# Products of the identity in TensorE's pauses, in a hybrid attention, recurrence and expert layer

## The chip, the cores and the metric

One core of one Trainium2 chip runs the whole program. The metric is the device time of one execution in microseconds (us), from runs of the same program; beside it stands one execution taken by the hardware profiler. TensorE has a clock that a throttle grants; the profile gives it as a share of 2.4 GHz, and it has two levels, 0.50 (1.2 GHz) and 1.00 (2.4 GHz).

## What is computed

One layer on x of 2048 tokens by 1024 columns, float32:

```
proj = x @ w_in                       # 2464 columns: c_q 256, c_kv 128, k_r 32, f, i, q, g 512 each
a = rms_norm(mla(c_q, c_kv, k_r))     # 8 heads, low-rank q and kv, rotary key, block-causal mask of 64
r = hgrn2(f, i, q, g)                 # 4 heads of 128, gated recurrence over chunks
h = layer_norm(ALPHA * x + concat(a, r) @ w_out)
moe: group = argmax(h @ w_router_group)          # 4 groups, top 1
     experts = top 2 of the 8 of that group      # 32 experts of 1024 x 512 (w1, w3) and 512 x 1024 (w2)
     y = (silu(h @ w1[e]) * (h @ w3[e])) @ w2[e], weighted by the gates and added
out = layer_norm(ALPHA * h + moe)
```

## The kernel before

The program is five blocks (stages) in sequence. Inside a block each engine has its own instruction list, in the order written, and engines meet through semaphores; at the end of a block all engines meet before any of them starts the next block. Float32 matrices are split into a high and a low part (type F32R), and a product is made of three such products (high by high, low by high, high by low). Products whose operands are plain F32 are one instruction in the code.

- **First stage, phase_a.** Eight spans of 256 tokens: projections, the chunkwise recurrence and its norm. Then the columns of the attention group are projected for all spans (project_four), and after each the sums of squares are taken with a matrix of ones (sums, L448; products at L453, bank pb or pu). The last thing on TensorE is sums(NS - 1). VectorE ends with the rotary factors and their product with the shared key (L777). Behind the block stand the clearing of semaphores and a barrier (L779, L780).
- **Second stage, phase_b.** TensorE first folds the shared key (L995, four products into S), then runs PROLOGUE, four preparations: keys, queries, values, queries of the first head (project, L1018; the values are the loop at L1033, four products of 128 columns per call, the queries two products of 512 columns). Then a loop over groups of steps: scores (L1051 to L1053, each of three products), transposes of the probabilities into T (L1063), the weighing of values (L1083), folds of the output (L1089), and the preparations for later heads. A score waits for the low part of the queries, which GpSimd writes (L1196) from what ScalarE (L1140) and VectorE (L1232) made of the prologue's banks. SyncE stores the outputs and waits until all have landed (L987).
- **Third stage, phase_c.** For each of eight pairs of 128-token tiles: w_out times attention and recurrence output (share, L1508), residual and layer norm on VectorE, the addition of the bias on GpSimd (L1664), and then the routing logits: route (L1537, eight transposes of h into H), copies of these by VectorE (L1673) and ScalarE (L1599), and logits (L1545, eight products of 36 columns into L). Its opening, begin (L1554), needs the split output weights: ScalarE writes the high part, VectorE the low part wo_lo (L1752 for the first four, L1749 for the last four, once their loads have landed); its first transposes are turn_a (L1527, into A[0]), whose low part VectorE writes behind wo_lo. The loop over pairs leaves logits(NT - 2, 0), route(NT - 1, 1) and logits(NT - 1, 1) for behind it. Rounds of the choice of experts for earlier pairs run on VectorE inside the loop.
- **Routing, phase_d.** A chain of small steps on VectorE (Chain: each waits for the one before) for the last four tiles and then for all: choose gives both, the mask of the two experts of each token; TensorE multiplies it with a triangle and with ones for the ranks (L1889, L1890), VectorE works out blocks and places up to at_blk (L1829, two halves), TensorE makes 32 products of 98 columns, the tokens (L1895, into tk), and one for the list of experts (L1898); VectorE makes at_gate of these (L1852, four instructions), and TensorE 32 products of 196 columns, the shares (L1902, into sh), which VectorE copies (L1875, L1876). SyncE meanwhile loads the first expert's weights, GpSimd gathers the first rows of h.
- **Expert stage and last norm, phase_e.** Rounds of 128 (and tails of 64) gathered tokens through one expert each, weights loaded for each round, then the last layer norm. Here TensorE is the engine with no idle time. At the opening it transposes the gathered rows (L2174) and those of the first tail (L2184, L2186).

The change adds its products to the lists of TensorE in the first four blocks. The instructions between which they stand: after sums(NS - 1) in phase_a; between the loop over PROLOGUE and the loop over groups, and behind the latter, in phase_b; ahead of begin(), between the loop of pairs and logits(NT - 2, 0), and at the end, in phase_c; and at four places in phase_d, ahead of each wait on steps but that for full, and at the end.

In the whole kernel t["ident"] is a plain F32 matrix of 128 by 128, t["ones"] as well. The values' projection is, for comparison, the same form of instruction as the added ones (F32, stationary 128x128, 128 columns):

```
for i in range(4):
    ins = pe.matmul(b[:, i * P:(i + 1) * P], t["ckvn"][:, (4 * c + i) * P:(4 * c + i + 1) * P],
                    wv[:, g], start=True, stop=True)
```

So is the product of keys and queries in the first stage, four heads for each of two halves of a span (L384):

```
for i in range(2):
    for h in range(HG):
        ins = pe.matmul(U[i][:, h * P:(h + 1) * P], key[:, h, i * P:(i + 1) * P],
                        ep[:, h, i * P:(i + 1) * P], start=True, stop=True)
```

Of the kernel before, what the change touches and what calls it, by code (L numbers as in the profile page):

```python
# [20 lines left out]
F32 = mybir.dt.float32  # L21
# [7 lines left out]
P = 128  # L29
# [73 lines left out]
def since(eng, sem, count):  # L103


    if not isinstance(count, int) or count > 0:
        eng.wait_ge(sem, count)


def shape_constants():  # L110
# [61 lines left out]
def phase_a(nc, t, d):  # L172

    with ExitStack() as ctx:
# [37 lines left out]
        O = psum("po")  # L212
# [35 lines left out]
        with nc.Block() as block:  # L248
# [53 lines left out]
            def _(pe):  # L302
# [143 lines left out]
                def sums(j):  # L446

                    pe.wait_ge(c_raw, 3 * j + 3)  # L448
                    pe.wait_ge(c_sq, 3 * j + 3)
                    b = PAIR[j % 2][0]  # L450
                    for n, (lo, hi) in enumerate(((0, 1), (1, 3))):
                        for k in range(lo, hi):
                            ins = pe.matmul(b[:, n * SPAN:(n + 1) * SPAN], t["ones"][:], csq[:, j % 2, k, :], start=(k == lo), stop=(k == hi - 1))  # L453
                    ins.then_inc(c_sum, 1)

                spans(pe, span)
                for j in range(1, NS):
# [9 lines left out]
                    sums(j - 1)  # L467
                    project_four(PAIR[j % 2], C_COLS, j % 2, c_done, 8, 16)
                sums(NS - 1)

            @block.scalar
            def _(act):
# [428 lines left out]
def phase_b(nc, t, d):  # L901


    with ExitStack() as ctx:
# [24 lines left out]
        T = [psum(f"pT{i}") for i in range(NTB)]  # L929
        O = [psum(f"pO{i}") for i in range(2)]  # L930
# [32 lines left out]
        with nc.Block() as block:  # L963
# [26 lines left out]
            def _(pe):  # L990
# [101 lines left out]

                for p in PROLOGUE:
                    project(p)
                for g in range(NGR + 2):
                    for half in range(2):
                        for n, i in scores_in(g, half):
                            score(n, i)
                        for s in slots_in(g, half):
                            if s < NU:  # L1100
                                turn(s)
                            if LAG <= s < NU + LAG:
                                weigh(s - LAG)
                            if s in FOLD_SLOT:
                                fold(FOLD_SLOT[s])
                        for p in preps_in(g, half):
                            project(p)

            @block.scalar
            def _(act):  # L1110
# [273 lines left out]
def phase_c(nc, t, d):  # L1384


    with ExitStack() as ctx:
# [21 lines left out]
        A = [psum(f"cA{i}") for i in range(1)]  # L1409
# [41 lines left out]
        with nc.Block() as block:  # L1451
# [39 lines left out]
            def _(pe):  # L1491
# [72 lines left out]
                def step(m, first):  # L1564
                    turn_a(m, 0)
                    project(m, 0)
                    if not first:
                        logits(m * 2 - 2, 0)
                        route(m * 2 - 1, 1)
                        if not isinstance(m, int) or m > 1:  # L1570
                            ranks(m - 2)
                    project(m, 1)
                    if not first:
                        logits(m * 2 - 1, 1)
                    route(m * 2, 0)
                begin()
                pe.wait_ge(c_loaded, 2 * 16)
                step(1, False)
                pe.wait_ge(r_consts, 3 * 16)
                with pe.Fori(2, STEPS) as m:  # L1580
                    step(m, False)
                logits(NT - 2, 0)
                route(NT - 1, 1)
                logits(NT - 1, 1)

            @block.scalar
            def _(act):
# [178 lines left out]
def phase_d(nc, t, d):  # L1766


    with ExitStack() as ctx:
# [14 lines left out]
        tk = ctx.enter_context(nc.psum_tensor("dT", [P, 512], F32))  # L1784
        sh = ctx.enter_context(nc.psum_tensor("dS", [P, 512], F32))
        xr = ctx.enter_context(nc.psum_tensor("dX", [P, 512], F32))
        listed = sem("d_listed"); copied = sem("residual_copied"); steps = sem("dve_d_steps"); exps = sem("d_exps_done"); ranks = sem("d_ranks")
        tokens = sem("d_tokens"); gates = sem("d_shares")
        idx_ready, gathered = t["idx_ready"], t["gathered"]
# [3 lines left out]
        with nc.Block() as block:  # L1793
# [90 lines left out]

            @block.tensor
            def _(pe):
                pe.wait_ge(steps, at["both"])
                b = s["both"][:].rearrange("p n e -> p (n e)")
                pe.matmul(rk[:, 0].rearrange("p n e -> p (n e)"), t["before"][:], b, start=True, stop=True)  # L1889
                pe.matmul(rk[:, 1].rearrange("p n e -> p (n e)"), t["ones"][:], b, start=True, stop=True).then_inc(ranks, 1)  # L1890

                for k in range(2):
                    pe.wait_ge(steps, at[f"at_blk{k}"])
                    for n in range(NT):
                        ins = pe.matmul(tk[:, 0:NBP], t["at_tok"][:, k, n], at_blk[:, k, n], start=(k == 0 and n == 0), stop=(k == 1 and n == NT - 1))  # L1895
                ins.then_inc(tokens, 1)
                pe.wait_ge(steps, at["full"])
                pe.matmul(xr[0:1, 0:P], full[:], t["ident"][:], start=True, stop=True).then_inc(listed, 1)  # L1898
                for k in range(2):
                    pe.wait_ge(steps, at[f"at_gate{k}"])  # L1900
                    for n in range(NT):
                        ins = pe.matmul(sh[:, 0:2 * NBP], t["at_row"][:, k, n], at_gate[:, k, n].rearrange("p f b -> p (f b)"),  # L1902
                                        start=(k == 0 and n == 0), stop=(k == 1 and n == NT - 1))
                ins.then_inc(gates, 1)

            @block.gpsimd
            def _(pool):
# [774 lines left out]
```

## Time and profile before

| what | value |
|---|---|
| median of 3 runs | 2335.55 us (2334.26 to 2335.8) |
| the profiled execution, its time | 2333.03 us |
| the profiled execution, its span (first to last instruction) | 2331.2 us |
| mean granted TensorE clock | 0.966 |
| PE busy | 2139.4 us, 92% |
| DVE busy | 1650.2 us, 71% |
| ACT busy | 1230.3 us, 53% |
| stages, start in the span | 0, 574.3, 1214.7, 1462.9, 1506.7 us |

PE is TensorE's matmuls, PEld its weight loads, DVE VectorE, ACT ScalarE, POOL GpSimd, SP SyncE. PEclk is the granted clock as a share of 2.4 GHz. A row of the timeline has the start, the time from the first start to the last end, engine, line, operation, what is written <- what is read, the shape and the number of records; in square brackets stands the idle time of the engine before it and what ended that. Records of matmuls overlap: the time of a run of them is the pace times their number, plus one latency.

### The profile page before, as it was taken

Reading aid. Unit: us, or ns where it says so; the run is one execution under the profiler, and the core shown is the slowest. Engines: PE = TensorE matmul, PEld = TensorE weight load, DVE = VectorE, ACT = ScalarE, POOL = GpSimd, SP = SyncE. Lnnn points to the kernel's source line nnn. Section 1 sums busy time; section 2 is a strip of 40 time slices with the busy share of each in tenths; the row PEclk is TensorE's granted clock in tenths of the full one; section 3 lists DMA queues with packets and bytes.
Section 4 is the critical chain, followed back from the end, with each engine's and each line's share of the span. In section 5 each row is a group of like instructions: output and inputs, shape, how many; then the busy total and the mean of one; then the engine's idle time right before and its main releaser. Section 6 shows DMA issues by size and latency. Waiting matters only on the chain. (4 is left out here: it accounts for less than half of the span.)

```text
span 2331.2 us, 40107 instructions
## 1 busy us (share of the span) xinstructions
PE 2139.4 (92%) x13020; PEld 1810.6 (78%) x13021; DVE 1650.2 (71%) x3068; ACT 1230.3 (53%) x2095; POOL 442.6 (19%) x256
## 2 busy tenths in 40 slices
PE   7999999999899999999989999499999999999980
PEld 6888888898677877787877888378888888888860
DVE  5444444465778878778775787778898877777756
ACT  5333333323666766677663221167676755656645
POOL 0000000000100000000001111124343435444436
PEclk9999999999899999999999999599999999999995
DMA  4111111333000000000034443489999988878937
GB/s 187 64 64 63 63 71 75 124 129 118 4 7 6 18 6 9 14 6 12 7 103 165 145 146 122 170 327 368 361 380 378 354 309 280 283 266 286 344 88 292
DMA packets 82215, 361.95 MB, mean 155 GB/s; under 512 B 25824, under 2 KB 37856, under 8 KB 65952
## 3 DMA queue, kind: packets, MB, share of 16 engines
q1 hardware_dynamic: 69136, 318.88, 36.2%
q0 software_dynamic: 11520, 41.16, 7.2%
q8 instruction: 68, 1.11, 0.2%
q10 hardware_dynamic: 1440, 0.37, 0.1%
q14 instruction: 51, 0.42, 0.1%
HBM read 291.97 MB, written 68.94 MB: 155 GB/s over the span
## 5 line engine op out<-in xcount | busy, mean ns | idle before, releaser
L2446 DVE TENSOR_TENSOR w_raw<-w_raw,w_hi 128x2048 fp32r<-128x2048 f32 x128 | 286.9, 2282 | 0.0
L1196 POOL TENSOR_TENSOR qT_lo<-q_raw,qT_hi 128x512 fp32r<-128x512 f32 x32 | 41.0, 1280 | 1124.4 <-ACT qT_hi L1140 1124.4
L1159 ACT CAST prT_hi<-pT 128x512 fp32r<-128x512 f32 (+1 forms) x288 | 162.6, 565 | 157.9 <-PE pT L1063 157.0
L1278 DVE TENSOR_TENSOR prT_lo<-pT,prT_hi 128x512 fp32r<-128x512 f32 (+1 forms) x288 | 188.1, 656 | 53.4 <-ACT prT_hi L1159 51.3
L2201 PE MATMUL eH<-w_hi,at_tok 128*128 128x512 f32 x512 | 206.9, 404 | 1.7 <-DVE at_tok L2439 1.7
L2202 PE MATMUL eH<-w_hi,at_tok 128*128 128x512 f32 x512 | 203.6, 398 | 0.0
L1269 DVE TENSOR_REDUCE mx<-pS 128x1 f32<-128x512 f32 (+2 forms) x320 | 191.2, 608 | 13.5 <-PE pS L1053 6.8
L2319 ACT CAST w_hi<-w_raw 128x2048 fp32r<-128x2048 f32 x64 | 122.6, 1916 | 73.9 <-issue 42.0
L99 POOL TENSOR_TENSOR cell<-cell 128x1 f32<-128x1 f32 x66 | 77.6, 1175 | 442.4 <-ACT y L2331 176.3
L1151 ACT ACTIVATE pr<-pS,nmx 128x512 f32<-128x512 f32 (+3 forms) x240 | 151.0, 639 | 14.4 <-DVE nmx L1273 14.0
L1063 PE MATMUL pT<-ident,pr 128*128 128x128 f32 x828 | 150.1, 275 | 8.3 <-DVE prT_lo L1278 8.0
L1051 PE MATMUL pS<-kT_hi,qT_hi 128*128 128x512 f32 (+2 forms) x320 | 137.2, 429 | 20.1 <-POOL qT_lo L1196 7.2
L2446 DVE TENSOR_TENSOR w_raw<-w_raw,at_row 128x2048 fp32r<-128x2048 f32 x62 | 139.2, 2286 | 13.2 <-ACT at_row L2310 12.6
L1083 PE MATMUL pO<-prT_hi,v_split 128*128 128x256 f32 x576 | 135.5, 317 | 2.3 <-DVE a_out L1294 2.3
L2208 PE MATMUL eH<-w_raw,at_tok 128*128 x512 | 129.7, 395 | 0.0
L305 PE MATMUL pb<-xT_hi,wf_hi 128*128 128x256 f32 x352 | 104.0, 295 | 22.0 <-DVE xT_lo L602 20.5
L2310 ACT CAST w_hi<-w_raw 128x2048 fp32r<-128x2048 f32 x64 | 119.3, 1922 | 0.0
L1083 PE MATMUL pO<-prT_lo,v_split 128*128 128x256 f32 (+1 forms) x576 | 118.4, 287 | 0.0
L1053 PE MATMUL pS<-kT_hi,qT_lo 128*128 128x512 f32 (+2 forms) x320 | 117.2, 366 | 0.0
L1052 PE MATMUL pS<-kT_lo,qT_hi 128*128 128x512 f32 (+2 forms) x320 | 117.1, 366 | 0.0
L2201 PEld LDWEIGHTS eH<-w_hi,at_tok 128*128 128x128 f32 x512 | 97.3, 190 | 25.2 <-issue 2.1
L2310 ACT CAST at_row<-w_raw 128x2048 fp32r<-128x2048 f32 x62 | 114.7, 1901 | 0.0
(429 smaller groups left out, 6017.2 us busy)
## 6 DMA issues: line engine op xcount, KB each, us to landing
w_raw<-in_w SPq DMA_DIRECT2D x96, 2048.0 KB, 12.5
xt<-in_x_t SPq DMA_DIRECT2D x9, 1024.0 KB, 7.8
xs<-in_x SPq DMA_DIRECT2D x8, 1024.0 KB, 4.8
scratch_h<-hp SPq DMA_DIRECT2D x16, 512.0 KB, 2.7
scratch_z<-hp SPq DMA_DIRECT2D x16, 512.0 KB, 3.6
fz<-scratch_z SPq DMA_DIRECT2D x16, 512.0 KB, 10.2
out<-fz SPq DMA_DIRECT2D x15, 512.0 KB, 4.2
scratch_xT<-xT_hi SPq DMA_DIRECT2D x7, 1024.0 KB, 3.9
```

The source lines that it names most:

```text
L1051: pe.matmul(b[:, 0:w], qh[:, slot, at], kh[:, key_slot(h), keys], start=True, stop=False)
L1063: ins = pe.transpose(b[:, m * P:(m + 1) * P], probs(n, i)[:, kt * P:(kt + 1) * P], t["ident"][:])
L1083: ins = pe.matmul(o, v[:, 2 * g + kk], w[:, u % RING, at], start=(g == 0 and m == 0), stop=(g == q and m == 3))
L1151: nc.scalar.activation(probs(n, i)[:, j * 512:j * 512 + w], S[S_AT["score", (n, i, j)] % 4][:, 0:w], ACT.Exp, scale=SCALE, bias=nmx[:, til ...
L1159: nc.scalar.copy(ph[:, u % RING, 0:w], T[u % NTB][:, 0:w]).then_inc(t_hi, 1)
L1269: v.tensor_reduce(mx[:, tile % 4, j:j + 1], b[:, 0:w], AX, ALU.max).then_inc(mx_part, 1)
L1278: v.tensor_tensor(pl[:, u % RING, 0:w], T[u % NTB][:, 0:w], ph[:, u % RING, 0:w].bitcast(F32), ALU.subtract).then_inc(t_lo, 1)
L2201: pe.matmul(H[:], xh[:, k, :], w.hi[:, k, :], start=(k == 0), stop=False)
L2202: pe.matmul(H[:], xl[:, k, :], w.hi[:, k, :], start=False, stop=False)
L2208: ins = pe.matmul(H[:], xh[:, k, :], lo[:, k, :], start=False, stop=(k == KT - 1))
L2310: nc.scalar.copy(w.hi[:, at], w.words(side)[:, at].bitcast(F32)).then_inc(w.hi_ready if half else w.hi_half, 1)
L2446: v.tensor_tensor(w.words(side)[:, at], w.words(side)[:, at].bitcast(F32), w.hi[:, at].bitcast(F32), ALU.subtract).then_inc(w.lo_ready if ...
```

## The change

A helper issues count products of a 128x128 matrix by itself into 128 columns of a bank. It is called at ten places with 14, 72, 14, 18, 28, 6, 40, 132, 60 and 20 products (404 in all), with the matrix of ones at the first and the identity at the others. A bank is given that nobody reads from then on or before its next writing; in routing a new one is allocated. No wait or semaphore is added and nothing is moved.

```diff
@@ -105,6 +105,12 @@
+def stay_warm(pe, bank, words, count):
+
+    for _ in range(count):
+        pe.matmul(bank[:, 0:P], words[:], words[:], start=True, stop=True)
@@ -467,6 +473,7 @@
                     project_four(PAIR[j % 2], C_COLS, j % 2, c_done, 8, 16)
                 sums(NS - 1)
+                stay_warm(pe, O, t["ones"], 14)
@@ -1092,6 +1099,7 @@
                 for p in PROLOGUE:
                     project(p)
+                stay_warm(pe, T[0], t["ident"], 72)
                 for g in range(NGR + 2):
@@ -1105,6 +1113,7 @@
                         for p in preps_in(g, half):
                             project(p)
+                stay_warm(pe, T[0], t["ident"], 14)
@@ -1573,15 +1582,18 @@
                     route(m * 2, 0)
+                stay_warm(pe, L, t["ident"], 18)
                 begin()
                 pe.wait_ge(c_loaded, 2 * 16)
                 step(1, False)
                 pe.wait_ge(r_consts, 3 * 16)
                 with pe.Fori(2, STEPS) as m:
                     step(m, False)
+                stay_warm(pe, A[0], t["ident"], 28)
                 logits(NT - 2, 0)
                 route(NT - 1, 1)
                 logits(NT - 1, 1)
+                stay_warm(pe, A[0], t["ident"], 6)
@@ -1784,6 +1796,7 @@
+        spare = ctx.enter_context(nc.psum_tensor("dV", [P, 512], F32))
@@ -1884,11 +1897,13 @@
             def _(pe):
+                stay_warm(pe, spare, t["ident"], 40)
                 pe.wait_ge(steps, at["both"])
                 b = s["both"][:].rearrange("p n e -> p (n e)")
                 pe.matmul(rk[:, 0].rearrange("p n e -> p (n e)"), t["before"][:], b, start=True, stop=True)
                 pe.matmul(rk[:, 1].rearrange("p n e -> p (n e)"), t["ones"][:], b, start=True, stop=True).then_inc(ranks, 1)
 
+                stay_warm(pe, spare, t["ident"], 132)
                 for k in range(2):
                     pe.wait_ge(steps, at[f"at_blk{k}"])
                     for n in range(NT):
@@ -1896,12 +1911,14 @@
                 ins.then_inc(tokens, 1)
                 pe.wait_ge(steps, at["full"])
                 pe.matmul(xr[0:1, 0:P], full[:], t["ident"][:], start=True, stop=True).then_inc(listed, 1)
+                stay_warm(pe, spare, t["ident"], 60)
                 for k in range(2):
                     pe.wait_ge(steps, at[f"at_gate{k}"])
...
                 ins.then_inc(gates, 1)
+                stay_warm(pe, spare, t["ident"], 20)
```

## Rows read from the trace of the kernel before

**Rows 1.** Windows by stage: us, PE, PEld, DVE, ACT, POOL busy (count), PEclk, DMA.

```profile
1462.90:1508.20 45.30, 15.66 (x70) 14.60 (x70) 36.15 (x111) 1.80 (x4) 5.01 (x3) 0.53 0.42 165
...
1530.00:2256.00 726.00, 725.93 (x3394) 588.31 (x3393) 575.95 (x536) 467.79 (x428) 304.42 (x170) 1.00 0.88 314
```

**Rows 2.** One line of the timeline, one of source line L384: F32 products, 128 columns.

```profile
581.22 1.05 PE L1034 MATMUL pS<-wv,ckvn 128*128 128x128 f32 x8
...
L384 PE MATMUL pu<-gate,key x128: 270/275/275, 61.7 to 460.0; 128*128 128x128 f32 x128
```

**Rows 3.** Timeline, end of the first stage.

```profile
570.01 1.53 PE L453 MATMUL pu<-csq,ones 128*128 128x256 f32 x6 [0.84 <-ACT csq L570]
...
574.32 0.43 DVE L1206 TENSOR_TENSOR krp<-krp,trig 128x256 f32<-128x256 f32 x1 [1.09 <-PEq L780]
```

**Rows 4.** Timeline behind the prologue, and the window behind it (columns as in 1).

```profile
582.11 1.88 PE L1031 MATMUL pS<-cqn,wq 128*128 128x512 f32 x4
...
591.19 0.45 PE L1051 MATMUL pS<-kT_hi,qT_hi 128*128 128x128 f32 x1 [7.20 <-POOL qT_lo L1196]
...
591.20:597.00 5.80, 5.80 (x18) 4.25 (x19) 3.34 (x12) 4.65 (x10) 1.27 (x1) 0.50 0.00 0
```

**Rows 5.** Second to third stage: timeline, and SyncE's waits of line L987.

```profile
1210.83 1.28 PE L1089 MATMUL pO<-stack,oT 128*128 128x64 f32 x8
...
L987 SPq EVENT_SEMAPHORE  x2: 17/22/28, 1213.6 to 1214.2; - x2
...
1214.74 0.09 DVE L1739 MEMSET carry<- 128x32 f32 x1 [2.25 <-PEq L963]
...
1217.65 0.76 PE L1508 MATMUL cM<-wo_hi,rts_hi 128*128 128x512 f32 x1 [5.54 <-DVE wo_lo L1752]
...
1229.40 2.47 DVE L1749 SCALAR_TENSOR_TENSOR wo_lo<-hT,ga,wo_hi 128x1024 fp32r<-128x1024 f32 x2
...
1230.54 0.60 PE L1527 MATMUL cA<-ident,an 128*128 128x128 f32 x4
```

**Rows 6.** Third stage's tail: timeline, and two windows (columns as in 1).

```profile
1445.82 1.87 PE L1545 MATMUL cL<-wr,hT 128*128 128x36 f32 x16
...
1452.19 3.63 PE L1545 MATMUL cL<-wr,hT 128*128 128x36 f32 x16 [3.60 <-DVE hT L1673]
...
1455.62 1.95 PE L1537 MATMUL cH<-ident,hp 128*128 128x128 f32 x8
...
1458.29 3.60 PE L1545 MATMUL cL<-wr,hT 128*128 128x36 f32 x16 [0.72 <-issue]
...
1448.60:1450.60 2.00, 0.00 (x0) 0.00 (x0) 1.57 (x5) 0.77 (x2) 0.00 (x0) 0.96 0.00 0
...
1452.20:1461.90 9.70, 8.97 (x40) 8.46 (x40) 0.89 (x2) 0.59 (x1) 1.66 (x1) 0.50 0.27 108
```

**Rows 7.** Timeline of routing and of the ends of its block.

```profile
1462.86 0.09 DVE L1804 MEMSET tok<- 128x34 int32 x1 [0.73 <-PEq L1451]
...
1468.77 0.79 PE L1889 MATMUL dW<-r_both,before 128*128 128x128 f32 x2 [6.87 <-DVE r_both L1337]
...
1470.09 0.19 DVE L1344 TENSOR_TENSOR r_rk<-dW,carry 128x32 f32<-128x32 f32 x1 [1.19 <-PE dW L1890]
...
1485.89 7.07 PE L1895 MATMUL dT<-at_blk,at_tok 128*128 128x98 f32 x32 [15.91 <-DVE at_blk L1829]
...
1493.07 0.16 DVE L1849 TENSOR_SCALAR idx<-dT 128x1 uint32<-128x1 f32 x1 [2.49 <-PE dT L1895]
...
1498.63 6.86 PE L1902 MATMUL dS<-at_gate,at_row 128*128 128x196 f32 x32 [5.16 <-DVE at_gate L1852]
...
1505.60 0.26 DVE L1875 COPY share<-dS 128x98 f32<-128x98 f32 x1 [0.89 <-PE dS L1902]
...
1506.73 0.37 DVE L2517 MEMSET marks<- 128x1 f32 x12 [0.57 <-PEq L1793]
```

**Rows 8.** Timeline, opening of the expert stage.

```profile
1528.20 0.33 PE L2184 MATMUL eZ<-ident 128*128 128x128 f32 x1 [2.49 <-DMA xg_tail<-scratch_h,idx]
```

## The prediction

> **What bounds the kernel now.** I read the windows by stage first. In the expert stage TensorE is busy for 725.93 of 726.00 us at clock 1.00: it is the bound there, and nothing before that stage is caught up in it. In the routing stage it is busy for 15.66 of 45.30 us at a granted clock of 0.53, while VectorE is busy for 36.15 [rows 1]. So routing is a serial chain of VectorE steps, with TensorE called in between. The change touches the pauses of TensorE at the openings of stages, in the third stage's tail and in routing. It can gain in one way only: the clock, which in those places is at the lower level (0.50 of 2.4 GHz, 1.2 GHz), stays at 2.4 GHz. It can lose in one way only: TensorE takes its instructions in order, so a fill that is longer than its pause makes the real product behind it late. The whole question is how long a product of the identity takes.
>
> **The price of one product.** Every filler is a plain float32 product, 128 columns wide, with a 128x128 stationary operand. The nearest row is the projection of values (four such products for each call of project): it shows 8 records in 1.05 us. A product is thus two records; the pace is (1.05 - 0.28)/7 = 0.11 us a record, 0.222 us a product. That is the pace of the high clock: 16 records at clock 0.50 take 3.63 us, 0.215 apart [rows 6]. The source line L384 says the same of the count: 128 records for 8 spans of 8 products [rows 2]. Ends: 0.111 us if the chip made one record of it (as a transpose is: four records in 0.60 us for four of them [rows 5]), 0.44 us at the low clock (twice as long). I take 0.222, the same form of instruction. The 404 fillers are then 90 us of TensorE.
>
> **First to second stage (14, 3.1 us).** The last sums end at 571.54; nothing stands behind them but the block's end. VectorE ends the stage at 573.23 and starts the next one 1.09 us later, at 574.32 [rows 3]. The fillers are issued from about 571.4 and end near 574.6. If a block's end waits for TensorE's last product, the next stage starts 1.4 us later; if not, TensorE is free at 574.5 against a start at 574.32, 0 to 0.2 us. No row has TensorE last at a block's end; I take +1.4, since those behind the end may reuse the bank. The clock was 1.00 here anyway: no gain.
>
> **After the prologue (72, 16.0 us).** The last prologue product ends at 583.99, and the first score starts at 591.19 after 7.20 us of idle time, released by GpSimd. The fillers are issued from 583.9 to 599.9: the first score is 8.7 us late. It and what follows ran at clock 0.50 until 597.0; at full clock half of the 5.80 us is saved, 2.9 us [rows 4]. All of the stage's work on ScalarE, VectorE and GpSimd hangs on scores, so nothing makes up for the delay: +5.8 (+8.7 if nothing is gained).
>
> **Second to third stage (14 and 18).** The last fold ends at 1212.11, and SyncE has its last output landed at 1214.2. The 14 fillers end near 1215.2: +1.0 (0 without a wait for them). The 18 behind the opening take 4.0 us, from 1214.7 to 1218.7, when the first product had started at 1217.65: 1.05 us late. TensorE came to its first transposes at 1230.54, and these are copied, but their low part waits for VectorE, whose wo_lo ends at 1229.40 + 2.47 = 1231.87, on a chain that has no TensorE in it [rows 5]. These 1.33 us hide the 1.05, and hide equally what a higher clock gives back of the 12.9 us between: 0 for the 18 and 0 for the clock. The cover is gone if TensorE is over 1.3 us late and the clock gives nothing back.
>
> **Third stage's tail (28 and 6).** TensorE stops at 1448.59; its next logits start at 1452.19. 28 fillers take 6.2 us and end at 1454.7, 2.5 us late. The logits that took 3.43 us at clock 0.50 take 1.7 (as at 1445.82); the transposes and the copies behind them took 2.67 us, of which half of eight transposes goes, 0.9; the last logits take 1.9 us instead of 3.6. They end at 1460.1 instead of 1461.89. The six fillers take 1.3 us, so TensorE ends at 1461.4 where VectorE had ended at 1462.13: -0.8 [rows 6, 7]. Bounds: -2 with no wait at the block's end, and see the second rival.
>
> **Routing (40, 132, 60, 20).** Each is set against the wait that stands there now [rows 7].
> - 40 take 8.9 us from the start of the stage; VectorE had both masks after 5.9 us (1462.86 to 1468.77): +3.0. The two rank products at full clock: from 1.32 to about 0.7 us, -0.6.
> - 132 take 29.3 us, issued from 0.3 us before VectorE resumes at 1470.09. VectorE needs 15.8 us to the first at_blk (1485.89). +13.2, the largest term. Then 32 products that took 7.18 us at clock 0.50 take 32 x 0.111 + 0.3 = 3.9: -3.3.
> - 60 take 13.3 us, and start about when VectorE has the tokens (1493.07); it needs 5.56 us for its at_gate (1498.63). +7.8. Then 32 products in 3.9 instead of 6.97 us: -3.1.
> - 20 take 4.4 us. VectorE had 0.55 us of work behind the shares (1505.60), and the next stage started at 1506.73, 1.13 after them. Now TensorE ends 4.4 us after, and the block's end adds 0.57: +3.8. Without a wait for it 0.
> Together +20.8. Nothing else fills these waits: VectorE's later steps stand behind TensorE's answers.
>
> **Opening of the expert stage.** Its clock rises earlier, but the gather of the first tail holds TensorE at 1528.20 for 2.49 us, and it comes by DMA [rows 8]: a TensorE that is early waits longer. 0, or -1 if the gather itself comes sooner.
>
> **Sum.** +1.4 + 5.8 + 1.0 - 0.8 + 20.8 = +28.2 us. The profiled execution has a span of 2331.2 us and a time of 2333.0, so 2361.2 there; the median of the runs, 2335.55, is 2.5 above it, and the forecast goes by the median: 2363.8 us.
>
> **Rivals.**
> First, the block's end does not wait for fillers: the terms of 1.4, 1.0 and 3.8 go, and the tail of the third stage gains about 1 more. +21 us, 2356.6. For it: bank and operand are read by nobody. Against it: a matmul in flight is an unfinished instruction like any other.
> Second, the clock falls again between the fills of the third stage's tail. In the profile the clock still stood at 0.96 in the two microseconds from 1448.6, after 2.8 us of narrow logits and transposes, and then fell; it stayed at 0.50 over 8.97 us of such instructions in the 9.7 us from 1452.2 [rows 6]. After the change 5.4 us of them stand between fill and fill. Should it fall there, the last logits take up to 1.7 us more, six fillers 1.3 more, and the first 4 us of the 40 run at half pace, 2 more: +33 us, 2368.8.
> The Trainium skill, TensorE: Matmul & The Clock Gate, section Part 4: PE-mode transpose, says that transposes do not count as a busy TensorE for the clock. By that rule this rival would be the case; the rows of the tail, which mix transposes with narrow products, agree, and those at 1445.8 (full pace after wide products) leave it open.
> Third, on the other side: a product of the identity takes one record, 0.111 us. Then the fills roughly fit: 72 take 8.0 us against 7.2, 132 take 14.7 against 15.8, 60 take 6.7 against 5.6. Terms: prologue 0.8 - 2.9 = -2.1; third stage's tail 1.7 + 0.9 + 1.8 - 0.3 = -4.1; routing -0.6 - 3.3 + 1.1 - 3.1 + 1.6 = -4.3. -10.5 us, 2325. For it: the counts fit the pauses at that price. Against it: both rows of two records for each product. On a straight line between the two prices (-10.5 at 0.111, +28.2 at 0.222) the time crosses that of before at 0.14 us a product; below that this rival holds.
> Fourth, the change does not do what it says: the fillers do not hold the clock. Each then takes 0.44 us beyond the first two or three microseconds; the 232 fillers ahead of the three waits of routing alone are 103 us against 27 of pauses. 2440 us or more. Against it: products of this form stood in the stretch in which the clock rose at 597.
>
> **How the numbers follow.** Forecast 0.62, first rival 0.10, second 0.17, third 0.06, fourth 0.03, something between the third and the forecast 0.02. Two measurements of this kernel can be told apart from about 0.2%, 4.7 us. Faster: the third, 0.06. Same: 0.02. Slower: 0.92. The range takes in the first two rivals, with 1.5 us below and 2 above for the unknown ends: 2355 to 2371.
>
> **What would show each step.** Right: twice as many records as fillers on line 113 (the helper), 0.222 us a product; first score near 600 plus 1.4; a VectorE wait of about 13 us for tokens that is not there now; clock 1.00 in the routing stage; a routing stage of 45 + 21 us between the third stage's end and the first cast of the experts; the expert stage unchanged in length. Wrong: one record a product; VectorE not waiting for at_blk's products; or a stage that starts while fillers still run, which decides between the forecast and the first rival.

## The result, and the profile of the changed kernel

The changed kernel takes 2366.6 us (median of 4 runs, 2363.85 to 2368.74) against 2335.68 beside it (2334.26 to 2338.13): a ratio of 1.0134, 95% interval 1.0119 to 1.0149. It is slower; the forecast was 2363.8 in a range of 2355 to 2371. The ratios here and below are taken over all runs and differ from the quotient of the two medians by up to 0.0005; one run of the kernel before, in the last of the groups used below, took 8490.69 us in the slow state and counts in no ratio. The profiled execution took 2365.4 us, with a span of 2363.6 and a mean granted clock of 0.982, where it was 0.966. The source line numbers of this kernel are 6 to 17 higher than those of the kernel before; the helper's product is L113.

The page: busy time, and the granted clock in 40 slices.

```profile
PE 2215.4 (94%) x13828; PEld 1887.9 (80%) x13829; DVE 1649.5 (70%) x3068; ACT 1230.3 (52%) x2095; POOL 442.6 (19%) x256
...
PEclk9999999999999999999999999999999999999995
```

VectorE, ScalarE and GpSimd do what they did; TensorE has 76 us more, and the kernel is 31 us longer. The records of TensorE are 808 more (13020 before), which is twice 404. The helper's source line, by bank, for three of the banks:

```profile
L113 PE MATMUL dV<-ident x504: 275/275/377, 1473.5 to 1537.7; 128*128 128x128 f32 x168
L113 PE MATMUL pT<-ident x172: 272/275/328, 586.8 to 1224.1; 128*128 128x128 f32 x172
...
L113 PE MATMUL po<-ones x28: 273/275/275, 573.0 to 576.0; 128*128 128x128 f32 x28
```

Twice as many records as products: 504 for 252 in routing, 172 for 86, 28 for 14. First, second and the opening of the third stage in the timeline (they answer to [rows 3, 4, 5]):

```profile
571.64 1.53 PE L459 MATMUL pu<-csq,ones 128*128 128x256 f32 x6 [0.84 <-ACT csq L577]
573.01 3.29 PE L113 MATMUL po<-ones 128*128 128x128 f32 x28
577.37 0.43 DVE L1215 TENSOR_TENSOR krp<-krp,trig 128x256 f32<-128x256 f32 x1 [2.51 <-PEq L787]
...
586.78 16.24 PE L113 MATMUL pT<-ident 128*128 128x128 f32 x144
602.78 0.31 PE L1058 MATMUL pS<-kT_hi,qT_hi 128*128 128x128 f32 x1
603.39 0.11 DVE L1276 MEMSET pS<- 64x64 f32 x1 [8.79 <-PE pS L1060]
...
1219.94 1.28 PE L1096 MATMUL pO<-stack,oT 128*128 128x64 f32 x8
1221.06 3.34 PE L113 MATMUL pT<-ident 128*128 128x128 f32 x28
1224.74 0.09 DVE L1751 MEMSET carry<- 128x32 f32 x1 [3.13 <-PEq L970]
```

VectorE, done with the first stage, now sits idle for 2.51 us at its end where it was 1.09, and for 3.13 us at the next end where it was 2.25. The tail of the third stage and routing (to be read against [rows 6, 7]):

```profile
1459.66 6.42 PE L113 MATMUL cA<-ident 128*128 128x128 f32 x56
1465.91 1.87 PE L1554 MATMUL cL<-wr,hT 128*128 128x36 f32 x16
1469.41 1.95 PE L1554 MATMUL cL<-wr,hT 128*128 128x36 f32 x16 [0.72 <-DVE hT L1685]
1471.19 1.58 PE L113 MATMUL cA<-ident 128*128 128x128 f32 x12
1473.46 9.17 PE L113 MATMUL dV<-ident 128*128 128x128 f32 x80 [0.68 <-PEq L1460]
1473.49 0.09 DVE L1817 MEMSET tok<- 128x34 int32 x1 [1.90 <-PEq L1460]
...
1482.91 29.64 PE L113 MATMUL dV<-ident 128*128 128x128 f32 x264
1483.18 0.19 DVE L1353 TENSOR_TENSOR r_rk<-dW,carry 128x32 f32<-128x32 f32 x1 [3.64 <-PE dW L1904]
...
1512.31 3.75 PE L1910 MATMUL dT<-at_blk,at_tok 128*128 128x98 f32 x32
...
1516.17 0.16 DVE L1862 TENSOR_SCALAR idx<-dT 128x1 uint32<-128x1 f32 x1 [12.50 <-PE dT L1910]
...
1516.30 13.66 PE L113 MATMUL dV<-ident 128*128 128x128 f32 x120
...
1529.72 3.80 PE L1918 MATMUL dS<-at_gate,at_row 128*128 128x196 f32 x32
...
1533.63 0.26 DVE L1888 COPY share<-dS 128x98 f32<-128x98 f32 x1 [5.83 <-PE dS L1918]
...
1538.34 0.37 DVE L2534 MEMSET marks<- 128x1 f32 x12 [4.15 <-PEq L1806]
```

The 32 products that took 7.07 and 6.86 us take 3.75 and 3.80: the clock is held. But VectorE stands still for 12.50 us until the first 32 are done. Windows (us, PE, PEld, DVE, ACT, POOL busy, PEclk, DMA) of routing and of the expert stage:

```profile
1473.50:1538.30 64.80, 64.50 (x574) 64.03 (x574) 35.61 (x96) 1.62 (x3) 4.31 (x2) 1.00 0.29 115
...
1562.00:2288.00 726.00, 725.73 (x3391) 587.95 (x3390) 575.89 (x536) 467.80 (x429) 304.45 (x170) 1.00 0.88 314
```

The clock is 1.00 all through routing (0.53 before, [rows 1]), VectorE's busy time is the same, and the stage is 64.85 us long instead of 43.87. Term by term, from the two profiled executions:

| stretch | forecast | measured |
|---|---|---|
| first stage's own part, not changed | 0 | +1.63 |
| end of first stage (14) | +1.4 | 4.31 to 5.73: +1.42 |
| next stage's start to the first score (72) | +8.7 | 16.87 to 25.41: +8.54 |
| first score to end of the last fold | -2.9 | 620.92 to 618.44: -2.48 |
| end of second stage (14) | +1.0 | 2.63 to 3.52: +0.89 |
| third stage to second transposes (18) | 0 | 17.96 to 17.55: -0.41 |
| from there to the third but last logits | 0 | 213.12 to 214.76: +1.64 |
| third stage's tail (28, 6) | -0.8 | 17.04 to 16.44: -0.60 |
| routing, to the first rank on VectorE (40) | +2.4 | 7.23 to 9.69: +2.46 |
| from there to the tokens (132) | +9.9 | 22.98 to 32.99: +10.01 |
| tokens to shares (60) | +4.7 | 12.53 to 17.46: +4.93 |
| shares to the expert stage (20) | +3.8 | 1.13 to 4.71: +3.58 |
| expert stage | 0 | +0.79 |
| sum | +28.2 | +32.4 |

The interval of the ratio is 27.8 to 34.8 us, which takes in both sums: only the stretches of the two traces tell them apart.

### The profile page after: what moved, and what is told of

Its sections match the earlier page's. It is cut to its first block and busy times, and to the rows that moved or that the text cites. A ratio compares the mean times of both kernels' runs of the same rounds, so it can differ in the third digit from the quotient of the medians.

```text
span 2363.6 us, 41723 instructions
## 1 busy us (share of the span) xinstructions
PE 2215.4 (94%) x13828; PEld 1887.9 (80%) x13829; DVE 1649.5 (70%) x3068; ACT 1230.3 (52%) x2095; POOL 442.6 (19%) x256
## 5 line engine op out<-in xcount | busy, mean ns | idle before, releaser
L1058 PE MATMUL pS<-kT_hi,qT_hi 128*128 128x512 f32 (+2 forms) x320 | 136.7, 427 | 13.2 <-ACT pr L1160 6.2
L2463 DVE TENSOR_TENSOR w_raw<-w_raw,at_row 128x2048 fp32r<-128x2048 f32 x62 | 139.1, 2285 | 13.2 <-ACT at_row L2327 12.6
L2218 PEld LDWEIGHTS eH<-w_hi,at_tok 128*128 128x128 f32 x512 | 97.4, 190 | 25.8 <-issue 2.7
L2219 PEld LDWEIGHTS eH<-w_hi,at_tok 128*128 128x128 f32 x512 | 97.5, 190 | 22.3
```

What stands on the lines that cost most here:

```text
L1058: pe.matmul(b[:, 0:w], qh[:, slot, at], kh[:, key_slot(h), keys], start=True, stop=False)
L2218: pe.matmul(H[:], xh[:, k, :], w.hi[:, k, :], start=(k == 0), stop=False)
L2219: pe.matmul(H[:], xl[:, k, :], w.hi[:, k, :], start=False, stop=False)
L2463: v.tensor_tensor(w.words(side)[:, at], w.words(side)[:, at].bitcast(F32), w.hi[:, at].bitcast(F32), ALU.subtract).then_inc(w.lo_ready if ...
```

## The experiments

All keep the changed kernel's code and set the ten counts, written here in their order (two block ends and the prologue first: 14, 72, 14; third stage 18, 28, 6; routing 40, 132, 60, 20). Each time is a median, beside runs of the kernel before on the same chip: 2335.6, 2335.55, 2334.94 and 2335.36 us in the four groups of runs.

**1. Routing alone, and all but routing.**

```diff
-14, 72, 14, 18, 28, 6, 40, 132, 60, 20
+ 0,  0,  0,  0,  0, 0, 40, 132, 60, 20    # e1
+14, 72, 14, 18, 28, 6,  0,   0,  0,  0    # e2
```

> The four fills of the routing stage alone (40, 132, 60, 20). Overrun theory (a fill costs its length, 0.222 us a product at full clock, less the pause that stood there, and gives back the low clock of the products behind it): +20.8 us as in the prediction, and about 2 more because the stage now starts at the low clock, where the first fillers take 0.44 us each: +21 to +24 us against the kernel before. Rival (the fills cost by being TensorE work: clock lost elsewhere, block ends, whatever their length against the pause): in proportion to their number, 252 of 404, +19 us, and a part of it outside the routing stage.

> The six fills outside the routing stage alone (14, 72, 14, 18, 28, 6). Overrun theory: +1.4 + 5.8 + 1.0 - 0.8 = +7.4 us, of which the first score after the prologue 8.5 us late from the start of its stage. Rival (cost in proportion to the number of fillers): 152 of 404, +12 us.

e1 took 2358.61 us (ratio 1.0095, 1.0080 to 1.0111), +23.0; its routing stage is 67.0 us, 23.1 over that of before, so nothing was lost elsewhere. The interval (18.7 to 25.9 us) takes in the rival's +19 as well; what refutes it is that no part of the cost lies outside routing. Its 40 products began at the low clock and took 11.32 us in place of 9.17. e2 took 2344.79 us (1.0040, 1.0025 to 1.0056), +9.2, between the two expectations, and its interval (5.8 to 13.1) takes in both. Its first score comes 25.50 us into its stage where it was 16.87, 8.6 later, as the first had it; experiment 6 finds the 1.6 us that its sum lacked. The two parts add up to 32.2 where the whole change costs 30.9.

**2. Counts cut to the pauses.** By the price of 0.222 us a product.

```diff
-14, 72, 14, 18, 28, 6, 40, 132, 60, 20
+ 0, 30,  8, 12, 15, 0, 24,  68, 22,  0    # e3
```

> Counts cut so that each fill is shorter than its pause at 0.222 us a product (0, 30, 8, 12, 15, 0, 24, 68, 22, 0). Overrun theory: no delay is left and the clock's gains stay: prologue -2.9, third stage's tail -4.4, routing -0.6 - 3.3 - 3.1 = -7.0, together -14 us (2321 where the kernel before has 2335.7); -10 if the clock falls once in the third stage's tail. Rival (cost in proportion to the number): 179 of 404, +14 us.

2329.18 us, ratio 0.9974 (0.9964 to 0.9985): faster than the kernel before, but by 6.4 us and not by 14. The third stage is 245.42 us long (248.12 before), and routing 42.31, only 1.56 less. Its timeline:

```profile
1459.36 8.46 PE L113 MATMUL dV<-ident 128*128 128x128 f32 x48 [0.97 <-PEq L1459]
1467.65 0.39 PE L1901 MATMUL dW<-r_both,before 128*128 128x128 f32 x2
...
1484.17 3.81 PE L1908 MATMUL dT<-at_blk,at_tok 128*128 128x98 f32 x32 [0.73 <-DVE at_blk L1840]
...
1494.46 3.86 PE L1916 MATMUL dS<-at_gate,at_row 128*128 128x196 f32 x32 [1.06 <-DVE at_gate L1863]
...
1500.57 0.26 DVE L1886 COPY share<-dS 128x98 f32<-128x98 f32 x1
```

The last 32 products end at 1498.32, and VectorE takes the shares at 1500.57, with no idle time ahead: it had its own work. This reading follows: the halved products are worth only what VectorE waited for them before, 2.49 and 0.89 us [rows 7]. Experiment 4 tests it. And the first fill, begun at the low clock, ran until 1467.7 where VectorE had the masks at 1465.2. The other large part of the shortfall, 1.5 us, is in the third stage (experiment 6).

**3. Transposes in place of products.** The same 404, each as a PE-mode transpose of the identity (the matrix of ones at the first place became the identity too, which the lines below do not show).

```diff
-        pe.matmul(bank[:, 0:P], words[:], words[:], start=True, stop=True)
+        pe.transpose(bank[:, 0:P], words[:], words[:])
```

> The same counts as transposes of the identity (one record each) in place of products (two). Overrun theory with a clock that transposes hold: a transpose takes 0.111 us, each fill is about as long as its pause, and the sum is that of the third rival, -10 us. With a clock that transposes do not hold (the Trainium skill, TensorE: Matmul & The Clock Gate, Part 4: PE-mode transpose): the clock falls during each fill, a transpose takes 0.21 us, the fills are about as long as now and the products behind them run at 0.50 as before the change: +1.4 + 8 + 1 + 3 + 13 + 8 + 4 and about 3 more at the end of the third stage, +35 to +42 us.

2330.16 us, ratio 0.9981 (0.9971 to 0.9991). Each transpose is one record, 132 of them in 14.57 us: 0.110 us each. In the first row below, the first fill of routing, and two windows, of its beginning and of the 132:

```profile
1460.81 5.90 PE L113 MATMUL dV<-ident 128*128 128x128 f32 x40 [0.68 <-PEq L1460]
...
1460.80:1464.80 4.00, 3.99 (x24) 4.00 (x25) 3.48 (x18) 1.25 (x1) 0.00 (x0) 0.65 0.76 231
1464.80:1466.70 1.90, 1.90 (x18) 1.67 (x16) 1.73 (x6) 0.00 (x0) 0.00 (x0) 1.00 1.00 423
1467.30:1481.80 14.50, 14.50 (x134) 14.34 (x132) 13.10 (x34) 0.00 (x0) 0.00 (x0) 1.00 0.79 336
```

TensorE ran nothing but transposes from 1459.3 to 1466.7; the clock fell soon behind the first of them, stood at 0.50 from 1460.8 to 1463.3, rose while the 40 ran, and stayed at 1.00 through 132 of them. It was also 1.00 through the 72 behind the prologue (8.02 us) and the 60 (6.77 us). The Trainium skill (TensorE: Matmul & The Clock Gate, Part 4: PE-mode transpose) says that they do not count as a busy TensorE; in this trace they did, and the measurement decides. It is one execution, and the fastest of nine: its mean granted clock is 0.982, that of the other eight 0.979 or 0.980, so that by my estimate the clock was low for some 9 to 14 us longer in them ((0.982 - 0.980) or (0.982 - 0.979), times 2326 us, over 0.5), at places that no trace shows. That transposes hold the clock in every execution is not shown. This run is also the kernel of the third rival of the prediction, with the counts as written at one record each. It gave -5.4 us, not -10.5. In its profile the prologue's place came to -2.1, the third stage's tail to -3.7 and routing to -3.8, where the rival had -2.1, -4.1 and -4.3; another 1.6 us went back in the third stage (experiment 6). The rest of the profile's difference is no cost of the fills that a run shows: the last sums of the first stage stand 2.45 us later and the expert stage is 0.9 us longer, both within what they vary.

**4. A first fill that is in time at either clock, and no fills at the third stage's opening.**

```diff
-0, 30, 8, 12, 15, 0, 24, 68, 22, 0    # e3
+0, 30, 8, 12, 15, 0, 14, 70, 24, 0    # e5
+0, 30, 0,  0, 15, 0, 14, 70, 24, 0    # e6
```

> Fills of 30, 8, 12, 15, 14, 70 and 24 products (the fit with 24 cut to 14 in front of the rank products, 68 and 22 raised to 70 and 24). Theory: in the fit, routing gained only 1.56 us because (a) its first fill began at the low clock (48 records in 8.46 us) and made the rank products 1.75 us late, and (b) VectorE has no more than 2.49 and 0.89 us of waits for the two sets of 32 products, so a faster set gives no more than that. With 14 the first fill is in time at either clock; routing should take 43.87 - 2.49 - 0.89 - 0.4 = 40.1 us and the kernel 2.2 us less than the fit: 2327.0. Rival: the shortfall lies in the block's end or in the fills behind the rank products; routing stays at 42.3 us and the time at 2329.2.

> As the run with 14, without the fills of 8 and 12 at the change from the second to the third stage. Theory (the prediction's 0 for this place): the chain of VectorE that ends with wo_lo hides whatever the clock gives there; the third stage is as long as with them within 0.5 us, and the time is 2327.0. Rival: a part of the 2.70 us that the fit gained in the third stage comes from its opening; without the two fills it is up to 1.5 us longer: 2328.5.

e5: 2327.61 us (0.9969, 0.9957 to 0.9981). e6: 2327.60 us (0.9967, 0.9955 to 0.9980). Routing is 40.06 and 40.07 us, as expected. In e5:

```profile
1459.24 6.14 PE L113 MATMUL dV<-ident 128*128 128x128 f32 x28 [0.98 <-PEq L1459]
1465.23 0.45 PE L1901 MATMUL dW<-r_both,before 128*128 128x128 f32 x2
...
1497.92 0.26 DVE L1884 TENSOR_TENSOR home<-d_away,d_pad 128x98 int32<-128x98 f32 x1
1498.21 0.26 DVE L1886 COPY share<-dS 128x98 f32<-128x98 f32 x1
...
1499.34 0.37 DVE L2531 MEMSET marks<- 128x1 f32 x12 [0.57 <-PEq L1804]
```

VectorE goes from its own work to the shares without a pause. The third stage is 245.28 us with the fills at its opening and 245.06 without: they are worth nothing in this pair, though the clock of the first eight microseconds is 1.00 with them and 0.64 without. Experiments 5 and 6 have kernels in which this cover did not hold.

**5. The changed kernel without the fills that end a block, and with half of the 132.**

```diff
-14, 72, 14, 18, 28, 6, 40, 132, 60, 20
+ 0, 72,  0, 18, 28, 6, 40, 132, 60,  0    # e7
+14, 72, 14, 18, 28, 6, 40,  66, 60, 20    # e8
```

> The changed kernel without the fills that stand last in a block (14 before the second stage, 14 before the third, 20 at the end of routing); 72, 18, 28, 6, 40, 132 and 60 stay. Theory: the block's end waits for TensorE's last product, so 1.4 + 1.0 + 3.8 = 6.2 us go: 2360.4. Rival: it does not, and the stages open when VectorE is done: no change, 2366.6.

> The changed kernel with 66 products in the place of 132. Theory: a product takes 0.222 us, 66 take 14.7 of the 15.8 us that VectorE needs there, and VectorE becomes the bound again: the whole overrun of 13.2 us goes and no more: 2353.4. Rival: a fill costs as it is long whatever VectorE does: 66 x 0.222 = 14.7 us less, 2351.9; or, at one record a product, 7.3 less, 2359.3.

e7: 2361.68 us (1.0109, 1.0093 to 1.0124). Shares to the next stage in its timeline:

```profile
1533.10 0.26 DVE L1886 COPY share<-dS 128x98 f32<-128x98 f32 x1 [5.82 <-PE dS L1916]
1534.22 0.37 DVE L2531 MEMSET marks<- 128x1 f32 x12 [0.57 <-PEq L1804]
```

1.12 us in place of 4.71; from the last sums to the second stage 4.31 in place of 5.73, from the last fold to the third 2.65 in place of 3.52. The block's end waits for products that nobody reads. These are 5.9 us, but the median is only 4.9 under that of the changed kernel (3.7 in the spans of the profiles), where 6.2 were expected. In its profile 0.8 us went back among the scores, where the clock fell once (0.72 in the six microseconds from 621), and 1.2 at the opening of the third stage: without the 14 ahead of it the 18 fillers met the low clock,

```profile
1223.01 5.88 PE L113 MATMUL cL<-ident 128*128 128x128 f32 x36 [2.60 <-PEq L969]
```

and VectorE, done with wo_lo, waited 0.88 us for the first transposes.

e8: 2351.77 us (1.0074, 1.0057 to 1.0090), 14.8 under the changed kernel; its four runs lie 8.4 us apart, so the time does not tell 13.2 from 14.7, but the trace does. TensorE now waits 1.17 us for at_blk, so VectorE is the bound again:

```profile
1472.50 11.48 PE L113 MATMUL dV<-ident 128*128 128x128 f32 x80 [0.68 <-PEq L1460]
1484.53 0.19 DVE L1353 TENSOR_TENSOR r_rk<-dW,carry 128x32 f32<-128x32 f32 x1 [5.96 <-PE dW L1904]
1500.34 3.81 PE L1910 MATMUL dT<-at_blk,at_tok 128*128 128x98 f32 x32 [1.17 <-DVE at_blk L1842]
...
1472.50:1474.50 2.00, 2.00 (x9) 2.00 (x10) 1.72 (x11) 1.25 (x1) 0.00 (x0) 0.50 0.68 135
```

But its routing is 53.90 us, 10.95 under the changed kernel and not 13.2. Up to here the two programs are the same, and yet in this execution the clock stood at 0.51 from 1470.5 to 1477.5, and the 40 products took 11.48 us for 9.17: with 0.55 more in the third stage's tail, 2.9 us. So the second rival's event is real. It is seen in this execution, and not in those of the changed kernel, e2 and e7, whose clock stayed at 1.00 there.

**6. Where the gain of the fitted kernels goes.** In every profile that has a fill behind the prologue, the clock falls to 0.50 once in the first two turns of the third stage: 18 to 24 us behind its start in e2, e3, e5 and e8, 32 to 38 us behind it in the other six. The changed kernel, e2 and e8 have the same instructions up to there and not the same place, so the place is not set by the program alone. The windows from 32 to 36 us behind the start of that stage, of the kernel before and of the changed one, each of its own trace:

```profile
1246.74:1250.74 4.00, 3.54 (x22) 3.16 (x23) 3.53 (x8) 1.79 (x4) 0.85 (x2) 1.00 0.71 251
```

```profile
1256.74:1260.74 4.00, 3.96 (x17) 3.58 (x18) 3.52 (x8) 1.98 (x4) 0.87 (x1) 0.59 0.81 275
```

Three of the four runs below test it, and whether the parts add up. e9 also asks for the opening of the expert stage.

```diff
-0, 30, 0, 0, 15, 0, 14, 70, 24, 0    # e6
+0, 30, 0, 0, 15, 0, 14, 70, 24, 8    # e9
+0,  0, 0, 0,  0, 0, 14, 70, 24, 0    # e10
+0,  0, 0, 0, 15, 0, 14, 70, 24, 0    # e11
+0, 30, 0, 0,  0, 0,  0,  0,  0, 0    # e12
```

> Fills of 30, 15, 14, 70 and 24, and 8 at the end of routing (the fit without the opening of the third stage, plus 8). Theory: VectorE still has 1.9 us of its own work when the last products of routing end, and 8 products are 1.8 us, so the block's end is not later (routing 40.1 us); the clock is then high at the opening of the expert stage, but the gather of the first tail holds TensorE there, so the stage is no shorter: the time of the same kernel without the 8, 2327.6, within 0.5. Rival: the low clock at 1500 to 1510 us costs the expert stage a part of its two slow microseconds: up to 1.5 us less, 2326.1; or the 8 end late, 0.5 to 1 us more.

> Only the three fills of routing, 14, 70 and 24; none before that stage. Theory: the gain of the fitted fills is a sum of independent places, of which routing gives 3.8 us (VectorE's waits of 2.49 and 0.89 and the half of 0.8 of the rank products), whatever stands ahead: routing 40.1 us, kernel 2335.6 - 3.8 = 2331.8. Rival: without the fills of the third stage's tail the clock is low at the start of routing and rises later, so that a part is lost: routing 41 to 42.5 us, kernel 2332.7 to 2334.2.

> Fills of 15, 14, 70 and 24 (third stage's tail and routing), none behind the prologue. So far all nine profiled kernels with a fill behind the prologue show a dip of the clock to 0.50 once in the first two turns of the third stage, and 214.6 to 214.8 us from its second transposes to the third but last logits; the three without one (the kernel before among them) show no dip and 213.1. Theory: the prologue's fill causes the dip. Without it the stretch is 213.1 us, the third stage 243.6, routing 40.1 and the time 2335.4 - 4.5 - 3.8 = 2327.1. Rival: the dip comes with any other fill or by chance: 214.7 and 245.1 us, and 2328.6.

> The fill of 30 behind the prologue alone. Theory: it saves 1.8 us in the second stage (first score to the next stage 621.5 us, where the kernels without it have 622.8 to 623.6) and gives 1.6 back by the dip in the third (214.7 us in the stretch where the kernel before has 213.1): nothing is left, 2335.2. Rival: no dip, 213.1 us, and 2333.6.

| run | us | ratio (95%) | first score to third stage | second transposes to logits | routing |
|---|---|---|---|---|---|
| before | 2335.55 | | 623.55 | 213.12 | 43.87 |
| e9 | 2327.15 | 0.9967 (0.9955 to 0.9979) | 621.57 | 214.75 | 40.05 |
| e10 | 2332.15 | 0.9986 (0.9977 to 0.9995) | 622.76 | 213.15 | 40.06 |
| e11 | 2327.39 | 0.9967 (0.9956 to 0.9978) | 622.82 | 213.11 | 40.02 |
| e12 | 2334.82 | 1.0001 (0.9992 to 1.0010) | 621.48 | 214.50 | 43.72 |

Windows of e12 and of e11 behind the start of the third stage:

```profile
1246.38:1250.38 4.00, 2.55 (x13) 2.55 (x13) 3.52 (x8) 1.35 (x3) 1.40 (x1) 0.62 0.44 178
```

```profile
1246.42:1254.42 8.00, 5.34 (x31) 4.45 (x30) 7.24 (x14) 1.79 (x4) 4.73 (x2) 1.00 0.54 187
```

The falls of e11 and e12 came out as the theory had them: none in e11, one in e12. Their times, 2327.39 and 2334.82, are near the theory's 2327.1 and 2335.2, but their intervals take in the rivals' 2328.6 and 2333.6 as well; the fifth column decides. So it is with e10 (2331.8 expected, 2332.7 and more by the rival): the 40.06 us of its routing decide. Over all fourteen profiles: the ten with a fill behind the prologue have 214.50 to 214.76 us in the fifth column, the four without 213.11 to 213.15. The fill of 30 saves 1.7 us of scores (621.39 to 621.57 in five profiles, 622.76 to 623.55 in the four without) and gives back 1.4 to 1.6 in the next stage, so that alone it is worth nothing (1.0001). e11, without it, is as fast as e6 and e9.

The opening of the third stage is not the same in all. In e12 the clock was at the low level for its first nine microseconds (first row, the first eight), TensorE came late to its first transposes, and VectorE had to wait behind wo_lo:

```profile
1214.38:1222.38 8.00, 5.10 (x12) 4.03 (x13) 6.06 (x8) 6.46 (x11) 0.00 (x0) 0.50 0.83 288
...
1228.92 2.47 DVE L1756 SCALAR_TENSOR_TENSOR wo_lo<-hT,ga,wo_hi 128x1024 fp32r<-128x1024 f32 x2
1232.50 0.69 DVE L1692 TENSOR_TENSOR anT_lo<-cA,anT_hi 128x512 fp32r<-128x512 f32 x1 [1.11 <-ACT anT_hi L1634]
```

This step begins 18.12 us behind the stage's start in e12, 17.94 in e7 and 17.57 in e11, and 16.60 to 17.12 in the eleven others, where VectorE goes to it without a pause. So the opening costs 0.5 to 1 us where the clock rises late, and whether a fill ahead of it would win that back in such an execution was not tried.

Routing alone is worth 3.8 us in its own stage and 3.3 in the ratio; the tail's 15 give the rest of e11 (13.11 us from its logits to routing, where the kernel before has 17.04). Its third stage is 244.6 us where 243.6 were expected; 0.45 of that is the opening. e9: 8 more products fit behind the last of routing (stage 40.05), and bring nothing; its expert stage is 825.76 us, against 825.93 in e6.

The fastest are e5, e6, e9 and e11, 0.31 to 0.33% under the kernel before and not to be told from each other. e11 has four fills, 123 products.

## Why the prediction was right

**The price.** Two records, 0.111 us each: 264 records take 29.64 us, so (29.64 - 0.28)/263 = 0.112. The row of the values' projection [rows 2] gave it, though it stands in another stage, with another source. The third rival fell here; e4 is a kernel at its price. The fourth fell with it: the fills stand at a clock of 1.00.

**Overrun against pause.** Each place of routing came out within 0.3 us of its term. e8 shows it from the other side: with 66 products TensorE waits 1.17 us for VectorE, and the fill costs nothing.

**The block's end waits** (1.4, 1.0 and 3.8 forecast; 1.42, 0.89 and 3.58 measured, taken back by e7): the first rival is refuted.

**The prologue.** 8.7 and -2.9 forecast, 8.54 and -2.48 measured. The three other profiles with 72 products put the second at -1.2 to -2.0, less the block's end, against the mean of the four without. One thing the prediction did not see is a second fall of the clock in the second stage, some 20 to 23 us behind the first score: it stands in the kernel before and in e1 and e10, not in the changed kernel, and in e7, the one with the -1.2. In the kernel before:

```profile
613.00:619.00 6.00, 5.62 (x27) 5.18 (x28) 4.47 (x14) 4.24 (x14) 0.60 (x1) 0.72 0.01 3
```

What it costs, and why the saving is not the whole 2.9, stays open.

**The zeros.** The opening of the third stage cost nothing in the changed kernel, and gave nothing in e5 against e6: in all three VectorE's chain to wo_lo ends last, as forecast. But the cover was mis-sized. VectorE's low part of the transposes also needs ScalarE's high part, which the prediction left out, and in the kernel before that ends at 1231.76, 0.1 us ahead of wo_lo and not 1.33:

```profile
1231.17 0.59 ACT L1627 CAST anT_hi<-cA 128x512 fp32r<-128x512 f32 x1 [1.15 <-PE cA L1527]
```

The zero came out because the clock gave back more than the 18 fillers cost: the first product starts 3.98 us into the stage where it was 2.91, and the first transposes 15.24 where it was 15.80. Where the clock gave less, nothing covered it: in e7 the transposes start 16.62 us into the stage, 0.82 later than before, and VectorE's step behind them 17.94, again 0.82 later. The expert stage's opening is worth nothing (e9 against e6).

**What was missed.** The sum was 4.2 us short in the profiled execution; the median was 2.8 over the forecast. 1.63 of it is no cost of the change: over the fourteen profiles the last sums start anywhere from 569.93 to 572.88 us, with the same instructions ahead. The step that failed is the zero for the third stage behind its opening: I took it that a stretch in which the clock stood at 1.00 would go on so. It measured +1.64, in the two turns in which the clock now falls. Most of the rest is the expert stage's +0.79, within what it varies over the profiles (824.40 to 825.93).

**The second rival** was given 0.17 for a fall between the fills of the third stage's tail. It did not happen in the changed kernel's profile, and did in e8's, later than thought: only the last six fillers and the 40 met it. Its price was put at about 5 us, and measured 2.9. Whether it is rare is open: the four executions of the changed kernel have mean granted clocks of 0.983, 0.982, 0.980 and 0.980, and the last two took longest (2367.79 and 2368.74 us against 2363.85 and 2365.4), but they have no trace. The reason that stood beside it, transposes that do not count, does not hold in e4's trace.

**For the gain.** My expectation for e3 counted the halved time of every product behind a pause as won, 7.0 us in routing. In routing it is won only up to VectorE's own wait: 3.8 us in e5, e6, e9, e10 and e11. The third rival's routing term, -4.3, came near this (-3.8 in e4) because overruns stood against it.

Not settled: why a fill that ends at about 592 us decides on a fall of the clock at about 1233 or 1247. e6, e9 and e12 have nothing new between the two. In the long stretch of scores the clock is at 1.00 from about 626 us on in all fourteen profiles; the fall ahead of that, between 614 and 626, does not sort them (e11 has neither it nor the later one, e7 has both). What differs is the moment at which everything behind it stands, by 1 to 2 us; no run varied that alone. That the prologue's fill brings the fall is a count, ten profiles against four, one execution of each kernel.

## What to carry to other kernels

Price a filler from a row of its own form before counting: here a float32 product is two records, and counts that fit at one record (as transposes, one record each, they saved 5 us in e4) cost 31 us at two. A fill is free only while it ends before the other engine has what the real product waits for; at the last place of a block it is free only while another engine still has work of its own there (8 products in e9, not 20), and what a held clock gives is bounded by how long the next engine now waits for the product, not by the product's halved time. Look for what a held clock does further on: here one fill's gain came back as a new fall in the next stage.

## What the runs showed of the hardware that was not expected

- In the one traced execution of e4, TensorE's clock rose and stayed up while it ran transposes of the identity alone (0.65 in the first four microseconds of 40 transposes, 1.00 from then on). The other eight executions had a lower mean clock and no trace.
- A float32 transpose of 128 by 128 is one record at a pace of 0.109 us (132 in 14.57 us, e4), and a float32 product of the same shape two at 0.112 (264 in 29.64 us).
- The same instructions can meet the clock at either level: before routing, behind the same tail, it was 1.00 in three profiled executions (the changed kernel, e2 and e7) and 0.51 in a fourth (e8).
- The end of a block waits for products that nobody reads: 14, 14 and 20 of them made the next stage start 1.42, 0.89 and 3.58 us later, and e7, without them, has 4.31, 2.65 and 1.12 us at the three places in place of 5.73, 3.52 and 4.71.
- Ten profiles of ten with a fill behind the prologue have a fall of the clock in the first 38 us of a stage that starts 620 us later, and none of the four without it has. The cause is open.
